# Products of constants in front of TensorE's waits, in a two-layer mixer, an attention block and a mixture of experts

## The reference

```
for l in 0, 1:                                   # first block
    mod = silu(c) @ ada_w[l] + ada_b[l]          # shift, scale and gain, six of 1024
    h = rmsnorm(x) * (1 + sc_m) + sh_m
    proj = h @ w_in[l]                           # q, k, v, latent, gates, state space
    x = x + g_m * (mix of three branches @ w_out[l])
    h = rmsnorm(x) * (1 + sc_f) + sh_f
    x = x + g_f * (silu(ua) * uv @ ffn_w_down[l])    # ua, uv: conv of h @ ffn_w_up[l]
# second block
x = x + attention(rmsnorm(x) @ w_in_2) @ w_out_2
h = rmsnorm(x); route each token to 2 of 32 experts    # router: h @ (1024 x 36)
x = rmsnorm(x + sum of gated experts(h))
```

## Time and profile before

| | |
|---|---|
| median of 3 runs | 1941.01 us (1939.08 to 1941.45) |
| the profiled execution | 1942.92 us, its span in the trace 1941.1 us |
| TensorE busy (PE) | 1861.5 us, 96% of the span |
| VectorE (DVE), ScalarE (ACT) busy | 625.1 us, 418.4 us |
| DMA | 443.25 MB, mean 228 GB/s |
| mean granted clock of TensorE | 0.983 |

### The profile page before, as it was taken

The page is one execution under the profiler, slowest core; times in us unless marked ns, Lnnn a source line. Parts: engine busy times, 40 slices in busy tenths (PEclk is TensorE's granted clock), DMA queues, the critical chain, the costliest instruction groups (busy, mean ns, idle before and its releaser), DMA issues.

```text
span 1941.1 us, 20268 instructions
## 1 busy us (share of the span) xinstructions
PE 1861.5 (96%) x8644; PEld 1300.5 (67%) x8644; DVE 625.1 (32%) x1149; ACT 418.4 (22%) x888; POOL 0.8 (0%) x9
## 2 busy tenths in 40 slices
PE   6999999999999999999999999999889999999996
PEld 2477787888888648788887888865764444434432
DVE  4352267333232335127642232024441111111112
ACT  3253122212110234312212121012421011011112
POOL 0000000000000000000000000000000000000000
PEclk9999999999999999999999999999989999999999
DMA  9753364265445665337245453453329999999993
GB/s 388 268 168 125 130 218 153 107 217 165 138 172 219 214 218 174 130 101 274 103 152 191 134 174 131 147 212 135 139 79 414 427 428 427 428 428 427 427 428 127
DMA packets 137433, 443.25 MB, mean 228 GB/s; under 512 B 8832, under 2 KB 58240, under 8 KB 123520
## 3 DMA queue, kind: packets, MB, share of 16 engines
q1 hardware_dynamic: 134912, 438.26, 59.8%
q10 hardware_dynamic: 2432, 3.71, 0.5%
HBM read 440.12 MB, written 1.84 MB: 228 GB/s over the span
## 4 chain that ended last, share of the span: by engine, by line
PE 91%; DVE 3%; ACT 2%; DMA 2%; issue 1%; DVEq 1%; ACTq 0%; SPq 0%
PE acc L709 36%; PE acc L1151 11%; PE acc L719 10%; PE aux L1190 6%; PE acc L987 4%; PE aux L987 4%; PE acc L1138 3%; PE acc L1008 3%; PE aux L645 2%; PE acc L1199 2%; PE aux L1199 2%; PE acc L963 1%; DMA ring<-in_w_in 1%; PE aux L655 1%; PE aux L808 1%; ACT area L1273 1%
## 5 line engine op out<-in xcount | busy, mean ns | idle before, releaser
L709 PE MATMUL acc<-hT,ring 128*128 128x256 f32 x2688 | 591.8, 382 | 7.1 <-ACT hT L1346 7.1
L709 PEld LDWEIGHTS acc<-hT,ring 128*128 128x128 f32 x2688 | 511.1, 191 | 83.0 <-issue 13.7
L719 PE MATMUL acc<-ring,hT 128*128 128x512 f32 (+1 forms) x384 | 167.1, 595 | 7.4 <-DMA ring<-in_w_in 3.8
L1151 PE MATMUL acc<-ring,yT 128*64 128x512 f32 x512 | 169.2, 594 | 0.0
L2113 DVE SCALAR_TENSOR_TENSOR area<-acc,vectors,area 128x255 f32<-128x255 f32 (+1 forms) x176 | 72.7, 475 | 213.2 <-ACT area L1526 211.5
L719 PEld LDWEIGHTS acc<-ring,hT 128*128 128x128 f32 x384 | 74.1, 195 | 93.9 <-issue 88.4
L1728 DVE SCALAR_TENSOR_TENSOR ring<-ring,cspread 128x1024 f32<-128x1024 f32 x80 | 93.1, 1220 | 67.8 <-DMA ring<-in_ada_rest 67.8
L2358 DVE TENSOR_TENSOR xT<-xT,acc 128x1024 f32<-128x1024 f32 x17 | 20.8, 1221 | 292.3 <-PE acc L1199 292.3
L1151 PE MATMUL acc<-area,yT 128*64 128x512 f32 x384 | 112.9, 594 | 0.0
L1151 PEld LDWEIGHTS acc<-ring,yT 128*64 128x64 f32 x512 | 52.4, 137 | 74.5 <-issue 74.5
L1273 ACT ACTIVATE area<-aux 128x512 f32<-128x512 f32 (+3 forms) x65 | 41.4, 676 | 230.7 <-PE aux L645 225.1
(11 more groups left out here) (383 smaller groups left out, 1941.6 us busy)
## 6 DMA issues: line engine op xcount, KB each, us to landing
ring<-in_w_in SPq DMA_DIRECT2D x34, 2048.0 KB, 9.5
ring<-in_ffn_w_up SPq DMA_DIRECT2D x44, 1024.0 KB, 7.7
ring<-in_ada_rest SPq DMA_DIRECT2D x20, 2048.0 KB, 7.9
ring<-in_w_up SPq DMA_DIRECT2D x17, 2048.0 KB, 18.6
ring<-in_w_down SPq DMA_DIRECT2D x17, 2048.0 KB, 18.2
ring<-in_w_gate SPq DMA_DIRECT2D x16, 2048.0 KB, 15.3
area<-in_w_up SPq DMA_DIRECT2D x12, 2048.0 KB, 18.9
area<-in_w_down SPq DMA_DIRECT2D x12, 2048.0 KB, 17.6
```

The lines of the kernel that those rows point to most:

```text
L709: mm = pe.matmul(acc[LU.buf[use]][:, SEQ * j:SEQ * j + SEQ], w[:, k, c0:c0 + P], x[:, k, :], start=(k == 0), stop=(k == n - 1))
L719: mm = pe.matmul(acc[LU.buf[use]][:, at:at + width], x[:, k, P * t:P * t + P], w[:, k, :], start=(k == 0), stop=(k == n - 1))
L1151: mm = pe.matmul(dst[CAP * e:CAP * e + CAP, :], xg[:, b, k, CAP * e:CAP * e + CAP], w[:, k, :], start=(k == 0), stop=(k == KT - 1))
```

## The change

A helper `keep_busy(count)` issues `count` products of the matrix of ones with the first 256 columns of the constants `kc`, 256 columns wide, into a part of PSUM that nobody reads at that time. It is called in front of TensorE's waits: 65 products in 19 places of the executed program. In front of the gather, the wait for `tok_out` now stands ahead of six products and the wait for `pm_ready` behind them. No other engine's program is changed.

```diff
+            def keep_busy(count, scratch=pmod[:, 256:512]):
+                for _ in range(count):
+                    pe.matmul(scratch, ones, kc[:, 0:256], start=True, stop=True)
...
             mm.then_inc(ada_done, 1)
+            keep_busy(8, acc[0][:, 0:256])
...
                     if n == 3:
+                        keep_busy(2)
                         pe.wait_ge(qkT_out, 4 * l + 1)
...
+                keep_busy(2)
                 pe.wait_ge(c_n, l + 1)
...
+                keep_busy(2)
                 pe.wait_ge(cT_out, l + 1)
...
                 norm_sum(4 * l + 2)
+                keep_busy(7, aux[:, 0:256])
...
                 norm_sum(4 * l + 4)
+                keep_busy(7 if l < DEPTH - 1 else 6, aux[:, 0:256])
...
             for u in range(8):
+                if u >= 6:
+                    keep_busy(1)
                 pe.wait_ge(p_exp, UNITS + u + 1)
...
+            keep_busy(3)
             outputs_transposes(0)
...
             pe.wait_ge(late_in, 16 * 8)
+            keep_busy(2)
...
                 if t:
+                    keep_busy(2, aux2[:, 0:256])
                     pe.wait_ge(h2_out, t)
...
+            keep_busy(1, aux2[:, 0:256])
             pe.wait_ge(og_ready, 1)
...
+            pe.wait_ge(tok_out, T)
+            keep_busy(6, aux2[:, 0:256])
             pe.wait_ge(pm_ready, 1)
-            pe.wait_ge(tok_out, T)
             gather(0, 0)
...
+                if q == PAIRS - 1:
+                    keep_busy(2, aux2[:, 0:256])
                 pe.wait_ge(he_ready, q + 1)
```

## The result

The changed kernel takes 1925.37 us (median of 4 runs, 1925.14 to 1927.81) against 1941.03 us for the kernel before (4 runs, 1939.08 to 1941.45). The ratio is 0.9919, with a 95% interval of 0.9907 to 0.993: faster by 0.8%, 15.7 us. The profiled execution took 1925.4 us, its span is 1923.6 us.

What follows compares the result with a forecast made beforehand. The chain of waits was taken as 91% TensorE, slowed by ten low-clock stretches. Gains summing to 19.6 us took 1942.9 to 1923.3, adjusted to 1922.8 us; range 1918.5 to 1929, the forecast's own 1918.5 to 1926.

Steps and rivals of the forecast that it cites:

- The clock is what the products buy: At TensorE's waits: products keep the clock at 1.00, regaining half the busy time in low stretches, at most 25.0 us.
- ten terms: Gains at first projection, two latent entries, four norms, last heads, router to gather, last pair: 0.6 to 3.1 us each.
- The products cost nothing at the full clock: At all filled waits: products of at most 0.45 us each fit inside, so the wait hides them.
- 3.6 in 3.8: First projection: eight products, 3.6 us, fit into the 3.8 us wait for the first weights.
- The router's fall stays, and the gather gets its clock back: Router: fall at 1428.58 stays, clock returns before the gather, which takes 3.73 us instead of 5.43: gain 1.7 us.
- The last heads: Last attention heads: VectorE stands in between, so gain 0.6 us, between 0 and 1.7.
- The sum: Whole kernel: the gains place by place add up to 19.6 us, from 1942.9 to 1923.3.
- My step from 1923.3 down to 1922.8: Whole kernel: allowance for the profiled execution lying 1.9 us above the median; 1921.4 was the other possibility.
- Rival 1: Latent entries, last heads, last pair: short waits aren't mended, 6.8 us of the gain lost, 1930 us; chance 0.10.
- Rival 2: State space stage: another engine, VectorE, takes the time through longer TensorE waits, 9.3 us less gain, 1932; chance 0.07.
- Rival 3: All filled waits: products don't hold the clock, run at the low clock and stick out 20.3 us, 1961; chance 0.03.
- Rival 4: Whole kernel: nothing happens, falls come at other places and cost the same, 1941 us; chance 0.03.

Runs made afterwards that it cites:

- Experiments 1 and 2: Changed kernel with products only at the first projection and four norms (1): 1933.44 us; with products only at all other places (2): 1932.70 us.
- experiment 4: Changed kernel with each product of 256 columns replaced by two of 32 columns: 1939.47 us.
- Experiment 5: Changed kernel with 16, 14, 14, 14, 12 products at the first projection and norms instead of 8, 7, 7, 7, 6: 1934.8 us.
- third experiment: Changed kernel with 5, 4, 4, 4, 3 products at the first projection and norms instead of 8, 7, 7, 7, 6: 1925.24 us.
- sixth kernel: Changed kernel without the 11 products from the router to the gather (2, 2, 1 and 6): 1926.97 us.
- eighth kernel: Seventh kernel with three more products in front of each of two state space waits in each layer: 1923.78 us.
- seventh kernel: Changed kernel with the first group's eight transposes put between the router's narrow logits products, and one product ahead of the second group: 1928.6 us.
- lean kernel: Ninth and tenth kernels together, with 5, 4, 4, 4, 3 products at the first projection and norms: 1921.69 us.
- ninth: Seventh kernel with eight products instead of one in front of the wait for the router's choice (og_ready): 1922.46 us.
- tenth: Changed kernel with four more products around the load of ada_w, ahead of the first projection: 1924.0 us.
- eleventh: Ninth kernel with the additions of the eighth and tenth: 1924.31 us.

## Why the prediction was right, and where it was off

- *The clock is what the products buy.* Right. All ten terms came out within 0.2 us of their size. Experiments 1 and 2 show for all places but the router that it is each place's own wait that sets its fall, and experiment 4 that it isn't the delay or the mere activity of TensorE that mends it.
- *The products cost nothing at the full clock.* Right in the profiled execution: the first projection begins at 38.61 in place of 38.53, and the products take 0.46 us each, where I had 0.45. Experiment 5 shows the other side: a product that doesn't fit costs its 0.44 us (6.21 for 14). And the fit at the first projection, "3.6 in 3.8", took one execution's wait for the wait: it is shorter when ada_w comes late, and then 0.7 to 1.8 us of the eight stick out.
- *The router's fall stays, and the gather gets its clock back.* Right in place and amount, 5.43 us to 3.84, 1.7 net. The way there was not quite as written: the fall came a little earlier, and the two products behind it ran at the low clock (1.75 us in place of 0.87), which took 0.6 us before it was regained.
- *The last heads.* 0.6 of a possible 1.7, as taken: VectorE stood in between.
- *The sum was too large by 2.1 us.* The sum left out that a fall could come where the profile of before had none. That is the step that failed: it took the ten stretches of one execution as the list of places. In the changed kernel's profile a fall at 925.67 took 1.5 us, in the state space part of layer 1, behind a wait of 0.84 us and 64-column products; the third experiment's profile has one at 310.6 instead, the same part of layer 0, worth 1.6. The other 0.6 are four terms at 0.1 to 0.2 too much. My step from 1923.3 down to 1922.8, for the execution's distance to its median, was half a microsecond in the wrong direction. The medians differ by 15.7 only, since the profiled execution of before lay 1.9 above its median and the changed kernel's lies at its own.
- *Rival 1* (short waits not mended) fell: no stretch at the latent entries, last heads or last pair, and the second kernel has 6.6 us of its gain from just these places. *Rival 2* fell with the 1.4 us at L913. *Rival 3* fell as a forecast of the whole, but its mechanism is real: where the clock is low when the products begin they stick out, by some 4.6 us at the first projection in one execution of the sixth kernel. *Rival 4* is what the narrow products gave, 1939.5 us.

What stays open: why the state space part falls in one profile and not in another with the same code there, and whether the products added there in the eighth kernel prevent it. Its gain against the changed kernel, 1.6 us, lies within the intervals.

## What to carry to other kernels

Ask for the granted clock in small steps before looking for idle time: a kernel whose chain is 91% TensorE can lose another 1% behind its waits, where no table of waits shows it, and each low stretch cost half of the busy time in it here. Put wide products of constants into about half of each wait, the short ones that stand close together too, on the side of the semaphore where nobody waits for them, and stop there: more brought nothing here, and what overshoots is paid in full, at twice the price if the clock is already low. A wait that ends with a load is not of one length; leave room for its shortest. Where narrow products must run for microseconds, place real wide work among them, and then look at the next wait, which the faster part makes longer.

## What the runs showed of the hardware

- Filling half was as good as filling all: 1.9 us of products and 1.82 us of nothing at a norm kept 1.00 (1925.24 against 1925.37 us).
- With products of 32 and 36 columns and transposes of 128, TensorE was busy in all of 20.4 us and stood at 0.50 for the whole time; the same kernel at the latent entry went from 1.00 to 0.52 behind 3.40 us of which 2.90 were busy.
- Making TensorE faster ahead of a wait can bring its clock down: with the transposes among the logits the wait for the experts' choice grew from 1.01 to 3.47 us and ended in a fall of 6.8 us (seventh kernel, at 1422.6; the eighth shows the same at 1421.5).
- The same code falls at different places in different executions. The state space part without products of its own fell in layer 1 in the changed and the lean kernel (925.6), the seventh (927.7) and the sixth (931.0), in layer 0 in the third (310.6), and in neither in the fifth, ninth and tenth, nor in the kernel before; the router's part fell in the eleventh, not in the ninth. A profile shows one sample of them, at some 1.6 us for a fall of 3.4, which is why sums over such stretches should be read as good to some 2 us.
